# A ring of seven buffers for the residual stream, three chunks of the next tile loaded a tile ahead

## The chip, the cores and the metric

The kernel runs on all 8 cores of one Trainium2 chip. Each core has five engines with an instruction stream of their own: TensorE (PE, matrix multiply), VectorE (DVE), ScalarE (ACT), GpSimd (POOL) and SyncE (SP), which here only issues DMA transfers. A core takes 4 of the 32 prompt sequences and 2 of the 16 sample streams; the cores exchange nothing. The metric is the device time of the slowest core in microseconds (us).

## The reference, cut to what matters

Two layers, each a mixer in two branches, then a normalisation. Biases, the split of `h` and the cache bookkeeping are left out here.

```python
h = x @ w_in                                   # 1024 -> 3072: u, v, g_A | glu_val, glu_gate, g_B
v = LN(gelu(v)) * a_ln_g + a_ln_b
s = tril(W_s[head]) @ v + bias                 # within chunks of 128 positions
y_a = gelu(u) * s * silu(g_A)
a = glu_val * sigmoid(glu_gate)
c = causal_depthwise_conv(a, width=31)
y_b = silu(LN(c)) * silu(g_B)
x_new = LN(ALPHA * x + concat(y_a, y_b) @ w_out)
```

Prompt: 32 sequences of 2048 positions, width 1024, float32. Sample: 16 streams of 32 positions. Outputs are both activations, the last 30 rows of the convolution's input, and the normalised `v` of the sample (`new_av_sample`, which needs `a_ln_g` and `a_ln_b` in full).

## The kernel before

A core works through 16 prompt tiles of 512 positions (4 sequences of 4 tiles), then one sample tile of 64. Each tile passes through both layers before the next begins. `Sched.emit` appends each instruction to its engine's list in the order of the Python code and adds a semaphore wait for whatever buffer it reads or overwrites; a DMA's wait stands in the issuing engine's list. So SyncE's list is strictly in order: what stands behind a waiting DMA waits as well.

A tile lives in four chunks of 128 positions, each a float32 buffer `xres` of 128x1024 (512 KB). Both layers update it in place: it is the residual, and at the end of layer 1 the result, stored from there to `yp` (L654). The buffers form a ring of five, `chunk_idx(t, j) = (4 * t + j) % 5`.

`tile_layer` does one layer of one tile. First, for each chunk j: ScalarE casts it to bf16 (L397) into `xbf`, which shares its memory with `yT`, so that the first cast waits until the output projection of the layer before has read `yT`; TensorE transposes it in 8 pieces (L400) into one of two PSUM buffers `ptr`; and VectorE (even j, L409) or ScalarE (odd j, L406) copies it to `xT`. When all four are there, the input projection runs: blocks of 512 output columns, 32 matmuls of 128x512 each (L417, L494), their weights in a ring of four slots `wr`, loaded by SyncE (L371) from a bf16 copy `wsc` that the first tile writes. Behind the first two blocks the convolution's input is spread by 16 small DMAs to `Sb` (L465). Gating, convolution and spatial matmuls follow, and the output projection (L622), chunk by chunk: `wo_front` adds it to the residual (L625) and sums its squares (ScalarE L629, GpSimd), `wo_back`, one chunk later, normalises it on VectorE (L647, L650). In layer 1 `wo_back` also puts the store L654 in SyncE's list.

The x loads (L678) are put in SyncE's list at two places: chunk 0 of tile t+1 ahead of tile t's layers, and chunks 1 to 3 of tile t+1 behind them. A load waits for the store of the chunk that had its buffer last:

```python
if t + 1 < n_tiles:
    emit_xload(t + 1, [0])
...                       # both layers of tile t, with its stores
if t + 1 < n_tiles:
    emit_xload(t + 1, [1, 2, 3])
```

`a_ln_g` and `a_ln_b` stand as broadcasts over 128 partitions in `avg` and `avb` (256 KB each a layer), loaded in the prologue (L277). `avb` is used in the prologue (L329), and both in the sample tile (L517, L519) only. `mhalf` holds -0.5 as the exponent of `rsqrt_pool` (L252), which reads at most four columns of it. The prologue loads parameters, builds the convolution's and the spatial weights, then loads the first x chunks.

Of the kernel before, what the change touches and what calls it, by code (L numbers as in the profile page):

```python
# [131 lines left out]
def build_nc(n_seq=4, seq_len=SEQ, n_samp=2):  # L132
# [29 lines left out]
    with es:  # L162
        sb = lambda name, shape, dt=F32: es.enter_context(nc.sbuf_tensor(name, shape, dt))
        S = Sched()
        for n in ["pe", "act", "dve", "pool", "sp", "d_c", "d_w0", "d_w1", "d_w2", "d_w3",
                  "d_s", "d_o0", "d_o1", "d_o2", "d_o3", "d_o4", "d_oc", "d_ov", "d_m", "d_pw0", "d_pw1", "d_pw2", "d_pw3", "d_pm", "d_ws0", "d_ws1", "d_ws2", "d_ws3", "d_x0", "d_x1", "d_x2", "d_x3", "d_x4", "d_m2"]:
            S.add_engine(n, es.enter_context(nc.semaphore("s_" + n)))

        xres = [sb(f"xres{i}", [128, D]) for i in range(5)]
# [20 lines left out]
        mhalf = sb("mhalf", [128, TT])  # L190
# [15 lines left out]
        avg = [sb(f"avg{l}", [128, WA]) for l in range(DEPTH)]  # L206
        avb = [sb(f"avb{l}", [128, WA]) for l in range(DEPTH)]
# [93 lines left out]
        for l in range(DEPTH):  # L301
# [27 lines left out]
            S.emit("dve", lambda e, l=l: e.tensor_copy(out=vbb, in_=avb[l][:]), reads=[f"avb{l}"], writes=CSQ4)  # L329
# [54 lines left out]
        def tile_layer(l, T, segs, xk, first_in_seq, last_in_seq, sample, hist_src, conv_out, y_out, av_out):  # L384
# [123 lines left out]
            for j in range(nj):  # L508
# [4 lines left out]
                if sample:  # L513
# [3 lines left out]
                    S.emit("dve", lambda e: e.tensor_tensor(out=vf32[:PT, :], in0=vf32[:PT, :], in1=avg[l][:PT, :], op=ALU.mult),  # L517
                           reads=["ostage", f"avg{l}"], writes=["ostage"])
                    S.emit("dve", lambda e: e.tensor_tensor(out=vf32[:PT, :], in0=vf32[:PT, :], in1=avb[l][:PT, :], op=ALU.add),  # L519
                           reads=["ostage", f"avb{l}"], writes=["ostage"])  # L520
# [148 lines left out]
        def chunk_idx(t, j):  # L669
            return (4 * t + j) % 5  # L670

        def emit_xload(t, js):
            b = t // tiles_per_seq
            ti = t % tiles_per_seq
            keys = []
            for j in js:
# [4 lines left out]
                keys.append(f"xres{idx}")  # L681
            return keys

        emit_xload(0, [0, 1, 2, 3])
# [101 lines left out]
```

How the kernel before makes its waits and increments, by code:

```python
    def replay(self, eng, handle):  # L113
        E = self.engs[eng]
        for kind, p in E.ops:
            if kind == "wait":
                e, v = p
                handle.wait_ge(self.engs[e].sem, v)
            elif kind == "op":
                p(handle)
            elif kind == "opinc":
                p(handle).then_inc(E.sem, 1)
            else:
                fn, d = p
                fn(handle).then_inc(self.engs[d].sem, 16)
```

## Time and profile before

| | |
|---|---|
| two runs | 3895.09 and 3959.07 us, median 3927.08 |
| the profiled execution | 3747.47 us |
| its span, slowest core (core 6) | 3745.9 us |
| spans of the eight cores | 3712.3 to 3745.9 us |
| busy share of PE, DVE, ACT, POOL | 68%, 39%, 37%, 20% |
| moved by DMA | 451.20 MB, mean 120 GB/s |

The profile shows the slowest core of one execution. A line number such as L397 is that of the kernel before. A row of the timeline has its start, its length, the engine, the line, the operation with the tiles it writes and reads, and in brackets how long the engine was idle before it and what ended that. `SPq` is the issuing of a DMA by SyncE; the transfer itself lasts longer than its issue. The timeline merges neighbours of one kind, with their count (x8).

### The profile page before, as it was taken

Reading aid. Unit: us, or ns where it says so; the run is one execution under the profiler, and the core shown is the slowest. Engines: PE = TensorE matmul, PEld = TensorE weight load, DVE = VectorE, ACT = ScalarE, POOL = GpSimd, SP = SyncE. Lnnn points to the kernel's source line nnn. Section 1 sums busy time; section 2 is a strip of 40 time slices with the busy share of each in tenths; the row PEclk is TensorE's granted clock in tenths of the full one; section 3 lists DMA queues with packets and bytes.
Section 4 is the critical chain, followed back from the end, with each engine's and each line's share of the span. In section 5 each row is a group of like instructions: output and inputs, shape, how many; then the busy total and the mean of one; then the engine's idle time right before and its main releaser. Section 6 shows DMA issues by size and latency. Waiting matters only on the chain.

```text
span 3745.9 us, 47469 instructions; the slowest of 8 cores (3712.3 to 3745.9 us)
## 1 busy us (share of the span) xinstructions
PE 2531.3 (68%) x15728; PEld 1171.4 (31%) x15728; DVE 1449.3 (39%) x2286; ACT 1396.4 (37%) x2285; POOL 752.2 (20%) x1186
## 2 busy tenths in 40 slices
PE   0465776867677676767677776768777677776753
PEld 0232333323233333323333333323333233333322
DVE  0144433334444342444434244443324444342442
ACT  0233444433443343334334343443433343343333
POOL 1032211112222121222212122221112222121221
PEclk9887888877788787878888787878778788887876
DMA  7764334342233434323343433243343333434324
GB/s 104 187 138 156 114 97 153 104 147 92 113 114 103 148 114 137 114 107 98 109 142 114 136 114 120 97 145 94 115 136 96 120 103 109 141 114 134 114 89 135
DMA packets 200509, 451.20 MB, mean 120 GB/s; under 512 B 62828, under 2 KB 147172, under 8 KB 165452
## 3 DMA queue, kind: packets, MB, share of 16 engines
q1 hardware_dynamic: 183436, 431.28, 35.6%
q0 software_dynamic: 16832, 16.90, 3.1%
q8 instruction: 128, 2.10, 0.2%
q14 instruction: 113, 0.93, 0.1%
HBM read 341.59 MB, written 51.59 MB: 105 GB/s over the span
## 4 chain that ended last, share of the span: by engine, by line
PE 50%; ACT 15%; issue 9%; DVE 8%; SPq 7%; DMA 6%; POOL 3%; DVEq 0%; ACTq 0%; POOLq 0%
PE pb L417 29%; PE pb L622 11%; SPq L465 4%; DVE yT L611 3%; PE pb L494 3%; DMA xres<-xp 3%; ACT cT L575 2%; ACT tmpf L629 2%; ACT csq L538 2%; ACT cbf L541 2%; ACT cT L535 2%; PE ptr L400 2%; DMA Sb<-a2T 2%; PE pb L547 2%; DVE xres L625 2%
## 5 line engine op out<-in xcount | busy, mean ns | idle before, releaser
L417 PE MATMUL pb<-xT,wr 128*128 128x512 bf16 (+1 forms) x5440 | 1250.2, 396 | 40.0 <-ACT xT L406 40.0
L417 PEld LDWEIGHTS pb<-xT,wr 128*128 128x128 bf16 x5440 | 544.2, 105 | 741.5 <-issue 239.2
L622 PE MATMUL pb<-wr,yT 128*128 128x512 bf16 (+1 forms) x2080 | 533.1, 424 | 280.2 <-DVE yT L611 276.8
L400 PE MATMUL ptr<-identb,yT 128*128 128x128 bf16 (+1 forms) x1040 | 124.4, 306 | 451.6 <-ACT yT L397 400.0
L629 ACT ACTIVATE tmpf<-xres 128x512 f32<-128x512 f32 x260 | 163.7, 630 | 651.7 <-DVE xres L625 639.0
L622 PEld LDWEIGHTS pb<-wr,yT 128*128 128x128 bf16 (+1 forms) x2080 | 220.4, 107 | 581.5 <-issue 393.8
L565 POOL TENSOR_TENSOR tT<-tT,tmpf 128x512 f32<-128x512 f32 (+1 forms) x136 | 179.2, 1345 | 833.7 <-ACT tmpf L564 833.7
L530 PE MATMUL pb<-Sb,Wst 128*32 128x512 bf16 (+1 forms) x4608 | 238.5, 365 | 102.9 <-DMA Sb<-a2T 59.8
L625 DVE SCALAR_TENSOR_TENSOR xres<-xres,pb 128x512 f32<-128x512 f32 x260 | 178.0, 684 | 322.6 <-PE pb L622 240.1
L503 POOL TENSOR_SCALAR sm<-mv 128x4 f32<-128x4 f32 (+1 forms) x34 | 8.0, 234 | 1406.1 <-DVE mv L501 1406.1
L452 DVE SCALAR_TENSOR_TENSOR a2T<-tmpf,pb 128x512 bf16<-128x512 f32 (+1 forms) x144 | 90.3, 632 | 510.1 <-PE pb L417 509.5
L500 DVE BATCH_NORM_STATS2 st6v<-tmpf 128x6 f32<-128x512 f32 (+1 forms) x130 | 90.3, 694 | 432.3 <-ACT tmpf L499 432.0
L400 PEld LDWEIGHTS ptr<-identb,yT 128*128 128x128 bf16 (+1 forms) x1040 | 101.5, 139 | 482.3 <-issue 481.3
L494 PE MATMUL pb<-wr,xT 128*128 128x512 bf16 (+1 forms) x1040 | 233.4, 383 | 0.0
L553 DVE SCALAR_TENSOR_TENSOR nt_a<-pb,nt_a 128x512 f32<-128x512 f32 (+1 forms) x34 | 22.6, 664 | 481.3 <-PE pb L549 415.2
L487 ACT ACTIVATE sgb<-pb 128x512 f32<-128x512 f32 (+1 forms) x136 | 77.5, 574 | 321.2 <-PE pb L417 321.2
L607 POOL TENSOR_TENSOR yT<-tmpf,tT 128x512 bf16<-128x512 f32 (+1 forms) x136 | 194.3, 1438 | 11.1 <-POOL yT L607 0.9
L397 ACT CAST yT<-xres 128x1024 bf16<-128x1024 f32 (+1 forms) x130 | 132.1, 1041 | 171.1 <-DMA xres<-xp 158.0
L530 PEld LDWEIGHTS pb<-Sb,Wst 128*32 128x32 bf16 x4608 | 122.7, 99 | 218.8 <-issue 122.5
L611 DVE TENSOR_TENSOR yT<-cT,sgb 128x512 bf16<-128x512 f32 (+1 forms) x136 | 185.5, 1383 | 7.7 <-DVE yT L611 0.8
L547 PE MATMUL pb<-cbf,onesb 128*128 128x512 bf16 (+1 forms) x136 | 58.8, 584 | 187.1 <-ACT cbf L541 187.1
L647 DVE SCALAR_TENSOR_TENSOR xres<-xres,psc,pg 128x1024 f32<-128x1024 f32 (+1 forms) x130 | 166.6, 1281 | 35.9 <-POOL psc L641 35.9
(89 smaller groups left out, 2556.9 us busy)
## 6 DMA issues: line engine op xcount, KB each, us to landing
wr<-wsc SPq DMA_DIRECT2D x256, 1024.0 KB, 5.8
Sb<-a2T SPq DMA_DIRECT2D x512, 135.0 KB, 3.1
xres<-xp SPq DMA_DIRECT2D x64, 512.0 KB, 6.3
yp<-xres SPq DMA_DIRECT2D x64, 512.0 KB, 2.7
wsc<-wr SPq DMA_DIRECT2D x16, 1024.0 KB, 11.0
wr<-w_in POOLq DMA_DIRECT2D x12, 1024.0 KB, 15.1
wr<-w_out POOLq DMA_DIRECT2D x4, 1024.0 KB, 17.6
pg<-post_ln_g SPq DMA_DIRECT2D x2, 512.0 KB, 7.0
```

What stands on the lines that cost most here:

```text
L400: S.emit("pe", [(lambda e, j=j, k=k, pi=pi: e.transpose(out=ptr[:, pi, 128 * k:128 * k + PT], in_=xbf[:PT, j, 128 * k:128 * k + 128], iden ...
L417: S.emit("pe", [(lambda e, k=k, m=m, pb=pb, wt=wt: e.matmul(pb[:, 0:T], lhsT=wt[:, k, 128 * m:128 * m + 128], rhs=xT[:, k, 0:T], start=(k ...
L465: S.emit("sp", [(lambda e, s=s, g=g, sg=sg: e.dma_start(out=Sv[32 * s:32 * s + 32, :, sg, 0:ncol].rearrange("p (m f) c -> p m f c", f=4)[: ...
L494: S.emit("pe", [(lambda e, k=k, j=j, pb=pb, wt=wt: e.matmul(pb[:PT, :], lhsT=xT[:, k, 128 * j:128 * j + PT], rhs=wt[:, k, :], start=(k == ...
L530: fns.append(lambda e, m=m, s=s, c0=c0, n=n, mm=mm, g=g, pb=pb: e.matmul(pb[32 * g:32 * g + 32, c0:c0 + n], lhsT=Wst[l][:, 4 * m + g, mm, ...
L565: S.emit("pool", lambda e: e.tensor_tensor(out=tTt[:, m, 0:T], in0=tTt[:, m, 0:T], in1=tp[:, 0:T], op=ALU.mult), reads=[tk, f"tT{m}"], wri ...
L607: S.emit("pool", lambda e, m=m, tp=tp: e.tensor_tensor(out=yT[:, m, 0:T], in0=tp[:, 0:T], in1=tTt[:, m, 0:T], op=ALU.mult), reads=[tk, f"t ...
L611: S.emit("dve", lambda e, m=m: e.tensor_tensor(out=yT[:, 4 + m, 0:T], in0=cT[:, m, 0:T], in1=sgb[:, m, 0:T], op=ALU.mult), reads=[f"cT{m}" ...
L622: S.emit("pe", [(lambda e, k=k, j=j, pb=pb, wt=wt: e.matmul(pb[:PT, :], lhsT=yT[:, k, 128 * j:128 * j + PT], rhs=wt[:, k, :], start=(k == ...
L625: S.emit("dve", lambda e, xr=xr, pb=pb, n2=n2, j=j: e.scalar_tensor_tensor(out=xr[:PT, 512 * n2:512 * n2 + 512], in0=xr[:PT, 512 * n2:512 ...
L629: S.emit("act", lambda e, xr=xr, tp=tp, n2=n2, j=j: e.activation(out=tp[:PT, :], in_=xr[:PT, 512 * n2:512 * n2 + 512], func=AF.Square, acc ...
L647: S.emit("dve", lambda e, xr=xr, j=j: e.scalar_tensor_tensor(out=xr[:PT, :], in0=xr[:PT, :], scalar=psc[:PT, j, 0:1], in1=pg[l][:PT, :], o ...
```

## The change

The ring has seven buffers (`% 7`). Chunks 0, 1 and 2 of tile t+1 are put in SyncE's list ahead of tile t's layers, chunk 3 behind them. To make room (two buffers of 4 KB a partition), the four tiles `avg` and `avb` go (8 KB a partition) and `mhalf` shrinks from 512 to 8 columns. `a_ln_b` is loaded in the prologue into the right halves of buffers 5 and 6, which the loads of chunks 1 and 2 of tile 1 overwrite; both `a_ln_g` and `a_ln_b` are loaded again ahead of the last tile's layers into two free buffers, where the sample tile reads them.

```diff
-        xres = [sb(f"xres{i}", [128, D]) for i in range(5)]
+        xres = [sb(f"xres{i}", [128, D]) for i in range(7)]
-        mhalf = sb("mhalf", [128, TT])
+        mhalf = sb("mhalf", [128, 8])
-        avg = [sb(f"avg{l}", [128, WA]) for l in range(DEPTH)]
-        avb = [sb(f"avb{l}", [128, WA]) for l in range(DEPTH)]
+        av_chunk = [5, 6]
-            pload(avg[l][:], a_ln_g[l].partition_broadcast(128), f"avg{l}")
-            pload(avb[l][:], a_ln_b[l].partition_broadcast(128), f"avb{l}")
+            pload(xres[av_chunk[l]][:, 512:1024], a_ln_b[l].partition_broadcast(128), f"xres{av_chunk[l]}")
...
         def chunk_idx(t, j):
-            return (4 * t + j) % 5
+            return (4 * t + j) % 7
...
             if t + 1 < n_tiles:
-                emit_xload(t + 1, [0])
+                emit_xload(t + 1, [0, 1, 2])
             else:
                 S.emit("sp", lambda e: e.dma_start(out=xres[sidx][0:n_samp * DEC_SEQ, :], in_=xs.rearrange("b t d -> (b t) d")),
                        writes=[f"xres{sidx}"], dma=f"d_x{sidx}")
+                for l in range(DEPTH):
+                    c = chunk_idx(n_tiles, 1 + l)
+                    av_chunk[l] = c
+                    S.emit("sp", [lambda e, c=c, l=l: e.dma_start(out=xres[c][:, 0:512], in_=a_ln_g[l].partition_broadcast(128)),
+                                  lambda e, c=c, l=l: e.dma_start(out=xres[c][:, 512:1024], in_=a_ln_b[l].partition_broadcast(128))],
+                           writes=[f"xres{c}"], dma=f"d_x{c}")
...
             if t + 1 < n_tiles:
-                emit_xload(t + 1, [1, 2, 3])
+                emit_xload(t + 1, [3])
```

Below, SyncE's list at the passage from tile 0 to tile 1, before the change. The number behind `xres` or `wr` is the buffer's; `s_d_o0` is the semaphore of the stores from `xres0`, `s_dve` and `s_pe` are the engines'. Here buffers 0, 1 and 2 take chunks 1, 2 and 3 of tile 1, and buffer 3 takes chunk 0 of tile 2:

```order
L654 DMA yp<-xres0 128x1024 [waits s_dve]
L654 DMA yp<-xres1 128x1024 [waits s_dve]
L654 DMA yp<-xres2 128x1024 [waits s_dve]
L654 DMA yp<-xres3 128x1024 [waits s_dve]
L678 DMA xres0<-xp 128x1024 [waits s_d_o0]
L678 DMA xres1<-xp 128x1024 [waits s_d_o1]
L678 DMA xres2<-xp 128x1024 [waits s_d_o2]
L678 DMA xres3<-xp 128x1024 [waits s_d_o3]
L371 DMA wr2<-wsc 128x4096 [waits s_d_ws2,s_pe]
```

And with the change:

```order
L653 DMA yp<-xres0 128x1024 [waits s_dve]
L653 DMA yp<-xres1 128x1024 [waits s_dve]
L653 DMA yp<-xres2 128x1024 [waits s_dve]
L653 DMA yp<-xres3 128x1024 [waits s_dve]
L676 DMA xres0<-xp 128x1024 [waits s_d_o0]
L676 DMA xres1<-xp 128x1024 [waits s_d_o1]
L676 DMA xres2<-xp 128x1024 [waits s_d_o2]
L676 DMA xres3<-xp 128x1024 [waits s_d_o3]
L369 DMA wr2<-wsc 128x4096 [waits s_d_ws2,s_pe]
```

Row by row it reads the same; what moved is the meaning of the buffers. Buffer 0 now takes chunk 3 of tile 1, and buffers 1, 2 and 3 take chunks 0, 1 and 2 of tile 2. The four loads wait for the same four stores as before, and the weight loads stand behind four of them as before.

ScalarE's list at the same passage, where it casts the chunks of tile 1 (`s_d_x0` is the semaphore of the loads into `xres0`), before the change:

```order
L397 CAST yT<-xres4 128x1024 [waits s_d_x4,s_pe]
L397 CAST yT<-xres0 128x1024 [waits s_d_x0]
L406 COPY xT<-ptr1 128x8x128 [waits s_pe]
L397 CAST yT<-xres1 128x1024 [waits s_d_x1]
L397 CAST yT<-xres2 128x1024 [waits s_d_x2]
L406 COPY xT<-ptr1 128x8x128 [waits s_pe]
```

And with the change:

```order
L395 CAST yT<-xres4 128x1024 [waits s_d_x4,s_pe]
L395 CAST yT<-xres5 128x1024 [waits s_d_x5]
L404 COPY xT<-ptr1 128x8x128 [waits s_pe]
L395 CAST yT<-xres6 128x1024 [waits s_d_x6]
L395 CAST yT<-xres0 128x1024 [waits s_d_x0]
L404 COPY xT<-ptr1 128x8x128 [waits s_pe]
```

The first cast reads buffer 4 in both. Chunks 1, 2 and 3 came from buffers 0, 1 and 2, all loaded at the passage; now chunks 1 and 2 come from buffers 5 and 6, loaded in the prologue, and only chunk 3 from buffer 0, loaded at the passage.

SyncE's list at the end of the prologue (`s_d_c`: parameter loads), before the change:

```order
L678 DMA xres0<-xp 128x1024
L678 DMA xres1<-xp 128x1024
L678 DMA xres2<-xp 128x1024
L678 DMA xres3<-xp 128x1024
L678 DMA xres4<-xp 128x1024
L367 DMA wsc<-wr0 128x4096 [waits s_d_pw0]
```

And with the change:

```order
L676 DMA xres0<-xp 128x1024
L676 DMA xres1<-xp 128x1024
L676 DMA xres2<-xp 128x1024
L676 DMA xres3<-xp 128x1024
L676 DMA xres4<-xp 128x1024
L676 DMA xres5<-xp 128x1024 [waits s_d_c]
L676 DMA xres6<-xp 128x1024 [waits s_dve]
L365 DMA wsc<-wr0 128x4096 [waits s_d_pw0]
```

Two loads are added ahead of the first tile's weight stores, one with a wait for the parameter loads and one with a wait for VectorE.

## Rows read from the trace of the kernel before

**Rows 1.** The page: its head, and the chain that ended last by engine and by line:

```profile
span 3745.9 us, 47469 instructions; the slowest of 8 cores (3712.3 to 3745.9 us)
...
PE 50%; ACT 15%; issue 9%; DVE 8%; SPq 7%; DMA 6%; POOL 3%; DVEq 0%; ACTq 0%; POOLq 0%
PE pb L417 29%; PE pb L622 11%; SPq L465 4%; DVE yT L611 3%; PE pb L494 3%; DMA xres<-xp 3%; ACT cT L575 2%; ACT tmpf L629 2%; ACT csq L538 2%; ACT cbf L541 2%; ACT cT L535 2%; PE ptr L400 2%; DMA Sb<-a2T 2%; PE pb L547 2%; DVE xres L625 2%
```

**Rows 2.** List of waits: engine, line, waited for, us in total, times, longest:

```profile
ACT yT L397 <- DMA xres<-xp: 158.0, 15, 11.5
```

**Rows 3.** Timeline of one passage: start, us, engine, line, tiles, [idle before, releaser]:

```profile
763.68 9.44 PE L622 MATMUL pb<-wr,yT 128*128 128x512 bf16 x43
...
777.84 1.03 ACT L397 CAST yT<-xres 128x1024 bf16<-128x1024 f32 x1
...
782.13 1.29 DVE L650 SCALAR_TENSOR_TENSOR xres<-xres,sm,pbb 128x1024 f32<-128x1024 f32 x1 [0.17 <-POOL a2T L438]
783.33 0.69 DVE L409 COPY xT<-ptr 128x1024 bf16<-128x1024 bf16 x1
783.91 2.87 SPq L678 DMA_DIRECT2D xres<-xp  x4
786.94 1.37 SPq L371 DMA_DIRECT2D wr<-wsc  x2
790.40 1.04 ACT L397 CAST yT<-xres 128x1024 bf16<-128x1024 f32 x1 [11.54 <-DMA xres<-xp]
...
791.59 1.01 PE L400 MATMUL ptr<-identb,yT 128*128 128x128 bf16 x8 [11.57 <-ACT yT L397]
792.69 1.01 ACT L406 COPY xT<-ptr 128x1024 bf16<-128x1024 bf16 x1 [1.25 <-PE ptr L400]
...
796.86 1.01 ACT L406 COPY xT<-ptr 128x1024 bf16<-128x1024 bf16 x1 [1.26 <-PE ptr L400]
...
798.01 4.42 PE L417 MATMUL pb<-xT,wr 128*128 128x512 bf16 x10 [1.25 <-ACT xT L406]
```

**Rows 4.** Timeline from layer 0 to layer 1 of one tile:

```profile
667.64 3.62 PE L622 MATMUL pb<-wr,yT 128*128 128x512 bf16 x16
...
685.42 4.94 PE L417 MATMUL pb<-xT,wr 128*128 128x512 bf16 x12 [1.25 <-ACT xT L406]
```

**Rows 5.** Timeline: first passage's cast; last passage's cast and first matmul:

```profile
364.06 1.04 ACT L397 CAST yT<-xres 128x1024 bf16<-128x1024 f32 x1 [11.42 <-DMA xres<-xp]
...
3403.54 1.04 ACT L397 CAST yT<-xres 128x1024 bf16<-128x1024 f32 x1 [10.12 <-DMA xres<-xp]
...
3411.16 16.91 PE L417 MATMUL pb<-xT,wr 128*128 128x512 bf16 x64 [1.25 <-ACT xT L406]
```

**Rows 6.** X loads (L678), issue to landing: all 64, then one passage's four:

```profile
DMA to landing us min/median/max: 4.5/6.3/8.9
...
DMA to landing us min/median/max: 6.4/7.4/7.7
```

**Rows 7.** Timeline of TensorE: the first 96 matmuls after two passages:

```profile
1236.65 22.24 PE L417 MATMUL pb<-xT,wr 128*128 128x512 bf16 x96 [1.25 <-ACT xT L406]
...
1449.06 23.54 PE L417 MATMUL pb<-xT,wr 128*128 128x512 bf16 x96 [1.25 <-ACT xT L406]
```

**Rows 8.** Stretch of the first tile: engines' busy us, clock, DMA share, GB/s:

```profile
113.00:135.00 22.00, 13.84 (x67) 7.15 (x68) 2.69 (x3) 9.32 (x11) 0.00 (x0) 1.00 0.76 309
```

**Rows 9.** Timeline of the prologue: a broadcast, VectorE's bias copy, the x loads:

```profile
15.94 0.43 SPq L277 DMA_DIRECT2D avg<-a_ln_g  x1
...
107.13 0.42 DVE L329 CAST csq<-avb 128x512 bf16<-128x512 f32 x1
...
108.64 4.41 SPq L678 DMA_DIRECT2D xres<-xp  x5
```

**Rows 10.** The two weight loads behind the x loads of [rows 3], to landing:

```profile
DMA to landing us min/median/max: 11.2/12.0/12.9
```

**Rows 11.** Spans and mean granted clock of the cores:

```profile
core 6: 3745.9 us, clock 0.816
```

More of the change, by code:

```diff
@@ L165, in build_nc @@
         for n in ["pe", "act", "dve", "pool", "sp", "d_c", "d_w0", "d_w1", "d_w2", "d_w3",
-                  "d_s", "d_o0", "d_o1", "d_o2", "d_o3", "d_o4", "d_oc", "d_ov", "d_m", "d_pw0", "d_pw1", "d_pw2", "d_pw3", "d_pm", "d_ws0", "d_ws1", "d_ws2", "d_ws3", "d_x0", "d_x1", "d_x2", "d_x3", "d_x4", "d_m2"]:
+                  "d_s", "d_o0", "d_o1", "d_o2", "d_o3", "d_o4", "d_o5", "d_o6", "d_x5", "d_x6", "d_oc", "d_ov", "d_m", "d_pw0", "d_pw1", "d_pw2", "d_pw3", "d_pm", "d_ws0", "d_ws1", "d_ws2", "d_ws3", "d_x0", "d_x1", "d_x2", "d_x3", "d_x4", "d_m2"]:
             S.add_engine(n, es.enter_context(nc.semaphore("s_" + n)))
-        xres = [sb(f"xres{i}", [128, D]) for i in range(5)]
+        xres = [sb(f"xres{i}", [128, D]) for i in range(7)]
         yT = sb("yT", [128, 8, TT], BF16)
@@ L328, in build_nc @@
                           for s2 in range(2)], reads=[f"WmT{l}"], writes=[f"WmTs{l}_0", f"WmTs{l}_1"], dma="d_m2")
-            S.emit("dve", lambda e, l=l: e.tensor_copy(out=vbb, in_=avb[l][:]), reads=[f"avb{l}"], writes=CSQ4)
+            S.emit("dve", lambda e, c=av_chunk[l]: e.tensor_copy(out=vbb, in_=xres[c][:, 512:1024]), reads=[f"xres{av_chunk[l]}"], writes=CSQ4)
             pbk, pkk = next_bank()
@@ L516, in tile_layer @@
                            reads=[tk, "sm1", "sm4"], writes=["ostage"])
[L517 to L520, printed above, removed]
+                    avc = av_chunk[l]
+                    S.emit("dve", lambda e, avc=avc: e.tensor_tensor(out=vf32[:PT, :], in0=vf32[:PT, :], in1=xres[avc][:PT, 0:512], op=ALU.mult),
+                           reads=["ostage", f"xres{avc}"], writes=["ostage"])
+                    S.emit("dve", lambda e, avc=avc: e.tensor_tensor(out=vf32[:PT, :], in0=vf32[:PT, :], in1=xres[avc][:PT, 512:1024], op=ALU.add),
+                           reads=["ostage", f"xres{avc}"], writes=["ostage"])
                     S.emit("sp", [(lambda e, s=s, c0=c0, n=n: e.dma_start(out=av_out[s], in_=vf32[c0:c0 + n, :]))
@@ L674, in emit_xload @@
             ti = t % tiles_per_seq
-            keys = []
             for j in js:
@@ L680, in emit_xload @@
                     writes=[f"xres{idx}"], dma=f"d_x{idx}")
-                keys.append(f"xres{idx}")
-            return keys
         emit_xload(0, [0, 1, 2, 3])
-        sidx = (4 * n_tiles) % 5
+        sidx = chunk_idx(n_tiles, 0)
         for t in range(n_tiles):
@@ L709, in build_nc @@
                        [nav[l, s] for s in range(n_samp)])
-        S.wait_all("sp", ["d_o0", "d_o1", "d_o2", "d_o3", "d_o4", "d_oc", "d_ov", "d_ws0", "d_ws1", "d_ws2", "d_ws3", "d_m", "d_m2", "d_s", "d_x0", "d_x1", "d_x2", "d_x3", "d_x4", "d_c", "d_pm"])
+        S.wait_all("sp", ["d_o0", "d_o1", "d_o2", "d_o3", "d_o4", "d_o5", "d_o6", "d_x5", "d_x6", "d_oc", "d_ov", "d_ws0", "d_ws1", "d_ws2", "d_ws3", "d_m", "d_m2", "d_s", "d_x0", "d_x1", "d_x2", "d_x3", "d_x4", "d_x5", "d_x6", "d_o5", "d_o6", "d_c", "d_pm"])
         with nc.allow_non_contiguous_dma(reason="tiny parameter gathers in the prologue"):
```

## The prediction

> **What bounds the kernel now.** I read the chain of work that ended last first. TensorE holds 50% of it, but one share is a plain transfer: loads of x (`DMA xres<-xp`), 3% of 3745.9 us [rows 1]. The list of waits says who stands there: ScalarE's cast at L397 waits 158.0 us in 15 waits, 11.5 us at the longest, for those loads [rows 2]. There are 16 prompt tiles, so 15 passages from one to the next: one wait for each, 10.5 us on average.
>
> The timeline of one passage shows its shape [rows 3]. TensorE's last matmul of the output projection ends at 763.68 + 9.44 = 773.12. The cast of chunk 0 runs at 777.84, since chunk 0 was loaded a tile ahead. Chunks 1 to 3 are asked for only at 783.91, because SyncE's queue is in order and they stand behind the fourth store of y, which needs VectorE's L650 of chunk 3 (it runs until 783.42). Chunk 1's cast starts at 790.40, 6.49 us after the request, with 11.54 us of idle before it. From there a serial tail runs: transposes, copy L406 at 792.69, the casts of chunks 2 and 3, transposes, copy at 796.86, and the first matmul of the next block at 798.01, 7.61 us after chunk 1's cast. The gap on TensorE's big matmuls is 24.89 us. The last passage repeats it: cast at 3403.54 after 10.12 us of idle, first matmul at 3411.16, again 7.62 us later; the first passage waits 11.42 us [rows 5]. From layer 0 to layer 1 inside a tile, where nothing is loaded, the gap is 685.42 - (667.64 + 3.62) = 14.16 us [rows 4]. So at most 24.9 - 14.2 = 10.7 us a passage, 160 us in all, hangs on the loads, and only if all of them were hidden.
>
> **The change, part by part.** *The ring of seven.* Chunks 0, 1 and 2 of the next tile are now loaded a whole tile ahead. Chunk 3 still stands behind the fourth store, but it is now the first of four loads there, in the place that chunk 1 had. The number of loads at that point of the queue is the same (four), and so is what they wait for, as the order shows. Weights for blocks 2 and 3 behind them are issued no later. So the passage becomes: casts of chunks 0 and 1 at 777.84 and right after it; chunk 1's copy on ScalarE; chunk 2's cast; VectorE's copy of chunk 0 at 783.33 as before (it is behind L650), then chunk 2's transposes and copy, about 1.9 us more (8 transposes take 792.69 - 791.59 = 1.10, a VectorE copy 0.69), done by 786. All of that is over before chunk 3 lands. I take chunk 3's cast to start where chunk 1's does now, 790.40. Behind it are the cast with its hand-over 791.59 - 790.40 = 1.19, transposes 1.10, and copy with hand-over 798.01 - 796.86 = 1.15 [rows 3], together 3.44 us in the place of 7.61. The gain is 4.17 us a passage, x 15 = 62.5 us.
>
> How sure is "lands where chunk 1 does"? The four loads of this passage took 6.4 to 7.7 us each from issue to landing, and all 64 took 4.5 to 8.9 [rows 6]. Four loads issued within 2.87 us with nearly one duration could mean that they share the engines evenly, so that the first gains nothing by being first. Bounds: landing 7.7 us after the request in place of 6.4 leaves 4.17 - 1.3 = 2.9 us a passage (43 us); 8.9 leaves 1.7 us (25 us). At best it comes after 4.5 us. Chunk 1's cast started 6.49 us after the request here, and on average 1.0 us sooner, since the mean wait is 10.5 us against 11.54 here; so 5.5 - 4.5 = 1 us more a passage (78 us). I take the middle, since contents and order of that stretch of the queue are unchanged. The Trainium skill, "DMA: Bandwidth & Descriptors", section "Queues, rings and completion order", says that each DMA engine takes descriptors in the order of its ring, but that a later transfer may finish before an earlier one. By its first half chunk 3 inherits chunk 1's place and the sum is the 62 us; by its second half the 43 us would be possible.
>
> *The clock at the start of the next block.* The first 10 matmuls after the passage take 4.42 us, 0.44 each [rows 3], the lower of the two levels (1.2 GHz); whole blocks of 96 take 22.24 to 23.54 us [rows 7]. What precedes a block now is 24 transposes in the last 7 us, afterwards only 8. No row shows a full-width block after so few. So the clock may rise later. Below: nothing. Above: the 1.3 us between the two blocks of [rows 7] at each passage, 20 us. I take 0.5 us, x 15 = 7.5 us lost, since both blocks of [rows 7] already begin slow after a gap.
>
> *Prologue.* Seven x loads stand there in place of five: +1 MB, early, while the first tile waits for its weights. From 113 to 135 us the queues moved 309 GB/s [rows 8], so 1 MB is 3.4 us of transfer; nothing if it fits between others, 3.4 if the weights wait behind all of it. I take 3. Two broadcasts of `a_ln_g` go away, 0.43 us of issue each [rows 9]: -1. The seventh load waits for the copy of `a_ln_b` in VectorE's prologue, which starts at 107.13, before SyncE issues the first x load at 108.64 [rows 9], so nothing; the smaller `mhalf` is read by the same few columns, so nothing.
>
> *The last tile.* In place of three x chunks and the sample's, it now issues one chunk, the sample's, and four broadcasts. That is less data before the weights; the broadcasts' issue time stands ahead of blocks 2 and 3. Those weights, issued from 786.94 on [rows 3], landed 11.2 to 12.9 us later [rows 10], so by 801; block 2 starts two thirds of 23.5 us after 798, at 814, and at 810 with the change. Cover 9 us; nothing charged, in any tile.
>
> Sum: 62.5 - 7.5 - 3 + 1 = 53 us. The profiled execution took 3747.47 us, so it would become about 3694. The two runs shown have the median 3927.08, 4.8% higher, for the same program; passages are made of ScalarE work and transfers, so I carry the 53 us over unscaled: **3874 us**, 1.4% less.
>
> **Rivals.**
> - *All of the load wait goes* (chance 0.04): gap 14.2 as between layers, 160 us less, 3767. Against it: chunk 3 is requested behind the fourth store, at 783.9, when the first matmul would already be near.
> - *No gain* (0.12): chunk 3 lands so late, or the clock rises so late, that under 20 us are left, 3910 to 3930. Landing at 8.9 us with the whole 1.3 us of clock gives 25 - 20 = 5 us. For it: the even durations of the four loads. Against it: in-order issue, and chunk 1 did come first.
> - *Slower* (0.07): TensorE's granted clock sinks because its work is packed more densely. Place: the matmul blocks, 50% of the chain, 1873 us, at a mean granted clock of 0.816 [rows 1, 11]. One per cent off that clock costs 19 us, so it decides from 2.8% on and is slower by 2% (79 us) from 7%. For it: the same program already ran 148 and 212 us above the profiled execution. Against it: the gap only shrinks from 24 to 20 us, and TensorE's work per us rises by 1.4%. The Trainium skill, "TensorE: Matmul & The Clock Gate", section "Seeing it yourself", warns of a current limiter that lowers a die's clock when several of its cores run dense matmuls; that would act this way. No row here shows it at work.
> - *The level of the runs moves* (0.13): a run of the changed kernel near the profiled execution's level gives 3694, whatever the ring does.
> - *My forecast*, a gain of 20 to 78 us at the level shown: 0.64.
>
> **The numbers.** At the level of the two runs the forecast's own range is 3849 to 3907, widened by their spread (3895 to 3959, 32 either way of the median). The lower end must reach the profiled level with the gain, 3680; the upper takes in the smallest gain, 3908. About 2% is what a measurement of this kernel can tell from no change. Faster by over 2%: 0.04 for the hidden wait, most of the level rival, and a little of the forecast's edge, 0.18. Slower by over 2%: the clock rival and some of a level that moves up, 0.07. Within: 0.75.
>
> **What would show it.** In the changed profile the cast's waits for x are 15 still, but of about 7 us each in place of 10.5 (the casts of chunks 1 and 2 and a copy, 3 us, and a hand-over have moved ahead of them); the wait is followed by one transposing round and the first matmul 3.4 us later, and the gap on big matmuls is near 20 us. A gap of 24 would say that chunk 3 comes late; a first block over 24 us, that the clock took it; a first tile longer by over 5 us, that the prologue cost more. I am wrong if the four loads land together or the granted clock differs by over 2%.

## The result

The changed kernel takes 3719.43 us in the median of 11 runs, the kernel before 3827.77 us in the median of 10. In about half of the runs of either kernel at least one die ran at a lower mean granted clock and held the time up; the comparison leaves such runs out, and all that follows leaves out such runs or such dies. It gives a ratio of 0.9753, 95% interval 0.9728 to 0.9778: faster by 2.5%. The profiled executions are 3747.47 us before and 3651.53 us after, 96 us less, where 53 us were forecast.

The page of the changed kernel, to be read beside [rows 1]: its head, and the chain by engine and by line. A line number of the changed kernel is one to two lower here than that of the same statement before (L395 for L397, L415 for L417, L676 for L678).

```profile
span 3650.0 us, 47476 instructions; the slowest of 8 cores (3620.0 to 3650.0 us)
...
PE 51%; ACT 15%; issue 9%; DVE 8%; SPq 7%; DMA 5%; POOL 4%; ACTq 0%; DVEq 0%; POOLq 0%
PE pb L415 31%; PE pb L621 11%; SPq L463 4%; DVE yT L610 3%; PE pb L492 3%; ACT cT L574 3%; DMA xres<-xp 2%; ACT tmpf L628 2%; ACT cT L534 2%; ACT csq L537 2%; ACT cbf L540 2%; DMA Sb<-a2T 2%; SPq L310 2%; DVE xres L624 2%; PE pb L546 2%
```

Its slowest core, beside [rows 11]. The mean granted clock of the slowest core rose from 0.816 to 0.831, and the mean over the eight cores from 0.821 to 0.833:

```profile
core 0: 3650.0 us, clock 0.831
```

The cast's wait for x, beside [rows 2]: still 15 waits, but 6.2 us each in place of 10.5:

```profile
ACT yT L395 <- DMA xres<-xp: 92.8, 15, 7.7
```

The timeline of one passage, beside [rows 3]:

```profile
1384.06 16.32 PE L621 MATMUL pb<-wr,yT 128*128 128x512 bf16 x64 [8.46 <-DVE yT L610]
...
1405.10 1.97 ACT L395 CAST yT<-xres 128x1024 bf16<-128x1024 f32 x2
...
1409.23 1.05 ACT L395 CAST yT<-xres 128x1024 bf16<-128x1024 f32 x1
1409.40 1.28 DVE L649 SCALAR_TENSOR_TENSOR xres<-xres,sm,pbb 128x1024 f32<-128x1024 f32 x1 [0.17 <-POOL a2T L436]
1410.60 0.68 DVE L407 COPY xT<-ptr 128x1024 bf16<-128x1024 bf16 x1
1411.18 2.92 SPq L676 DMA_DIRECT2D xres<-xp  x4
...
1416.00 1.04 ACT L395 CAST yT<-xres 128x1024 bf16<-128x1024 f32 x1 [5.72 <-DMA xres<-xp]
...
1417.18 1.01 PE L398 MATMUL ptr<-identb,yT 128*128 128x128 bf16 x8 [4.74 <-ACT yT L395]
1418.29 1.01 ACT L404 COPY xT<-ptr 128x1024 bf16<-128x1024 bf16 x1 [1.25 <-PE ptr L398]
...
1419.44 5.77 PE L415 MATMUL pb<-xT,wr 128*128 128x512 bf16 x18 [1.25 <-ACT xT L404]
```

The output projection ends at 1384.06 + 16.32 = 1400.38 and the next block starts at 1419.44, a gap of 19.06 us where [rows 3] had 24.89. Chunks 0 and 1 are cast at 1405.10 and chunk 2 at 1409.23, before SyncE issues its four loads at 1411.18. Only chunk 3 is waited for. Its cast starts 4.82 us after the request, and the first matmul 3.44 us behind the cast: exactly the tail that the forecast had made of [rows 3].

From the timelines of all eight cores, the sums over the 15 passages and the tiles behind them (mean over the cores, us):

| part | before | after | after - before |
|---|---|---|---|
| first tile, both layers | 345.4 | 341.0 | -4.4 |
| gap at the passage | 357.5 | 291.9 | -65.6 |
| layer 0: first 96 matmuls and what stands among them | 367.2 | 354.6 | -12.6 |
| layer 0: from there to the statistics' matmuls, with them | 363.1 | 362.9 | -0.2 |
| layer 0: second block, spatial matmuls, waits | 366.5 | 364.7 | -1.8 |
| layer 0: output projection | 241.1 | 239.0 | -2.1 |
| layer 1, all of it | 1552.0 | 1546.5 | -5.5 |
| sample tile | 126.0 | 125.9 | -0.1 |

So 66 of 92 us are the gap, and 22 us come out of stretches that the change does not touch, 12.6 of them out of the first matmul blocks, which have the same instructions and now take less time. The other 4 us are the first tile's.

A view that the forecast had not used shows how. These are the issues of the y stores by SyncE, one group at the end of each tile, so their distances are the time from tile to tile. Before, at the ends of tiles 3 to 6 (counted from 0):

```profile
995.14 13.92 SPq L654 DMA_DIRECT2D yp<-xres  x4
...
1210.46 13.61 SPq L654 DMA_DIRECT2D yp<-xres  x4
...
1421.86 13.92 SPq L654 DMA_DIRECT2D yp<-xres  x4
...
1636.82 13.92 SPq L654 DMA_DIRECT2D yp<-xres  x4
```

215.3, 211.4 and 215.0 us. And after:

```profile
980.97 13.93 SPq L653 DMA_DIRECT2D yp<-xres  x4
...
1188.96 13.92 SPq L653 DMA_DIRECT2D yp<-xres  x4
...
1397.16 13.93 SPq L653 DMA_DIRECT2D yp<-xres  x4
...
1605.36 13.92 SPq L653 DMA_DIRECT2D yp<-xres  x4
```

208.0, 208.2 and 208.2 us. Times of ordinary tiles (those that do not end a sequence; 88 on the eight cores) do not spread evenly. Before, 54 are nearest to 215.0 and 30 to 211.6 us; after, 73 to 208.2 and 13 to 211.6. They move in steps of 3.4 us.

### The profile page after: what moved, and what is told of

It is laid out like the page before. It is cut to its first block, busy times and chain, and to the rows that moved or that the text cites. A ratio compares the mean times of both kernels' runs of the same rounds, so it can differ in the third digit from the quotient of the medians.

```text
span 3650.0 us, 47476 instructions; the slowest of 8 cores (3620.0 to 3650.0 us)
## 1 busy us (share of the span) xinstructions
PE 2498.8 (68%) x15728; PEld 1163.1 (32%) x15728; DVE 1451.4 (40%) x2286; ACT 1395.9 (38%) x2285; POOL 753.9 (21%) x1186
## 4 chain that ended last, share of the span: by engine, by line
PE 51%; ACT 15%; issue 9%; DVE 8%; SPq 7%; DMA 5%; POOL 4%; ACTq 0%; DVEq 0%; POOLq 0%
PE pb L415 31%; PE pb L621 11%; SPq L463 4%; DVE yT L610 3%; PE pb L492 3%; ACT cT L574 3%; DMA xres<-xp 2%; ACT tmpf L628 2%; ACT cT L534 2%; ACT csq L537 2%; ACT cbf L540 2%; DMA Sb<-a2T 2%; SPq L310 2%; DVE xres L624 2%; PE pb L546 2%
## 5 line engine op out<-in xcount | busy, mean ns | idle before, releaser
L415 PE MATMUL pb<-xT,wr 128*128 128x512 bf16 (+1 forms) x5440 | 1227.0, 391 | 40.0 <-ACT xT L404 40.0
L415 PEld LDWEIGHTS pb<-xT,wr 128*128 128x128 bf16 x5440 | 538.9, 104 | 723.9 <-issue 188.9
L398 PE MATMUL ptr<-identb,yT 128*128 128x128 bf16 (+1 forms) x1040 | 125.9, 306 | 386.1 <-ACT yT L395 286.4
L649 DVE SCALAR_TENSOR_TENSOR xres<-xres,sm,pbb 128x1024 f32<-128x1024 f32 (+1 forms) x130 | 167.7, 1290 | 24.2 <-POOL psc L632 16.9
```

The source lines that it names most:

```text
L398: S.emit("pe", [(lambda e, j=j, k=k, pi=pi: e.transpose(out=ptr[:, pi, 128 * k:128 * k + PT], in_=xbf[:PT, j, 128 * k:128 * k + 128], iden ...
L415: S.emit("pe", [(lambda e, k=k, m=m, pb=pb, wt=wt: e.matmul(pb[:, 0:T], lhsT=wt[:, k, 128 * m:128 * m + 128], rhs=xT[:, k, 0:T], start=(k ...
L649: S.emit("dve", lambda e, xr=xr, j=j: e.scalar_tensor_tensor(out=xr[:PT, :], in0=xr[:PT, :], scalar=sm[1][:PT, j:j + 1], in1=pbb[l][:PT, : ...
```

## The experiments

Theory A: the gain comes from when chunks are asked for. Theory K: beside that, the blocks' time depends on where a stretch of matmuls begins against changes of the granted clock that come at their own times, so tile times move in steps and a gap's change does not show as itself. Rivals: the memory layout does it; the clock simply comes back sooner after a shorter gap (S); time is simply added and taken away (L). The experiments ran on four chips; the kernel before, run again on each, had medians of 3739 to 3748 us there. Differences between two experiments are therefore read from the times of tiles and blocks first. Three of the kernels below rest on one execution each (four copies on the changed kernel, eight copies, two copies with the filler), two on two each (the early load without copies and with two), and one on four cores of one execution.

### The ring and the prologue alone

To the changed kernel, with the loads put back in their old places:

```diff
-                emit_xload(t + 1, [0, 1, 2])
+                emit_xload(t + 1, [0])
...
-                emit_xload(t + 1, [3])
+                emit_xload(t + 1, [1, 2, 3])
```

> Seven buffers and the new prologue, but the loads of x at the two old places (chunk 0 of the next tile ahead of the layers, chunks 1 to 3 behind them). Theory A (the gain comes from when chunks are asked for, plus the clock; the prologue gives its own 4.6 us): the passages between tiles are as in the kernel before, big-matmul gap near 23.8 us, 15 waits of the cast of about 10.5 us; the first x load is issued about 4.6 us earlier than before on average over the cores; time 0.998 of before. Rival B (the memory layout or the ring's size itself speeds something up, such as the first matmul block): the first block of 96 matmuls is shorter by 0.8 us at each passage with the gap unchanged, time 0.99 of before.

Ratio to before 0.9994 (0.9971 to 1.0017). The row of the cast's wait:

```profile
ACT yT L395 <- DMA xres<-xp: 156.7, 15, 11.8
```

The sum of the gaps is 355.8 us (before 357.5), that of the first blocks 367.0 (before 367.2). So the seven buffers, their addresses and the smaller tiles do nothing that shows at the passages, and rival B falls. The first x load is issued at 100.7 us on average over the cores, against 107.0 before. But in the other runs with the new prologue this average lies anywhere from 99.7 to 108.2 us, and in the one other run with the old prologue at 105.4. The first tile takes anywhere from 337 to 346 us in the runs with the new prologue, and 345 and 342 us in the two with the old one. The 4.4 us of the table are inside that spread, so whether the prologue gains anything stays open.

### Five buffers, loads between the stores

Each load of chunk j stands right behind the store of chunk j. To the kernel before:

```diff
                     S.emit("sp", lambda e, xr=xr, j=j: e.dma_start(out=y_out[j], in_=xr[:PT, :]), reads=[xkey], dma="d_o" + xkey[-1])
+                    after_store(j)      # emit_xload(t + 1, [j]) for j >= 1
...
-            if t + 1 < n_tiles:
-                emit_xload(t + 1, [1, 2, 3])
```

> The kernel before with its five buffers and its prologue; only each load of chunk j (1, 2, 3) of the next tile now stands right behind the store of chunk j, in place of all three behind the fourth store. Theory A (what counts is that one chunk alone is still asked for behind the fourth store): gap near 19.5 us as in the changed kernel, time 0.976 to 0.98 of before. Rival C (the two more buffers are needed, since a load waits for the landing of a store just issued): gap stays over 22 us, time 0.99 to 1.0 of before.

Ratio 0.9807 (0.9749 to 0.9865), where rival C had said 0.99 to 1.0. One passage of it, SyncE, ScalarE and TensorE (L660 is the store, L685 the load, L403 the cast, L423 the first block):

```profile
991.64 0.33 SPq L660 DMA_DIRECT2D yp<-xres  x1
992.07 3.19 SPq L685 DMA_DIRECT2D xres<-xp  x2
...
998.68 1.05 ACT L403 CAST yT<-xres 128x1024 bf16<-128x1024 f32 x1 [3.98 <-DMA xres<-xp]
...
1002.13 23.26 PE L423 MATMUL pb<-xT,wr 128*128 128x512 bf16 x96 [1.25 <-ACT xT L412]
```

The last store is issued at 991.64, chunk 3's load right behind it, its cast runs at 998.68, and the block starts 3.45 us later. The mean gap is 19.8 us. The mechanism of the forecast is shown, and it does not need the two buffers: what counts is how many chunks stand behind the fourth store. The rival, a wait for a store just issued, costs little: 45 waits of the cast for x with 106.1 us in all, where the changed kernel has 15 with 92.8. Of 88 ordinary tiles 49 take 208.2 us and 38 take 211.6. With a gap larger by 0.3 us than in the changed kernel, 25 more tiles stand on the higher step.

### Chunk 3 asked for early as well

To the changed kernel, the load of chunk 3 right behind the second store; it needs the buffer of the first:

```diff
+                    after_store(j)      # emit_xload(t + 1, [3]) for j == 1
...
-            if t + 1 < n_tiles:
-                emit_xload(t + 1, [3])
```

> The changed kernel, with the load of chunk 3 right behind the second store of y (it needs the first one's buffer) in place of behind the fourth. Theory A: no chunk is waited for any more, the gap falls to the 14.2 us that stand between the two layers of a tile, 5.3 us less than in the changed kernel at 15 passages, 80 us: ratio to before near 0.955. If the clock's rise is a matter of where a stretch of matmuls begins (theory K), the 80 us come out as anything from 51 to 102 us, a whole number of steps of 3.4 us at most passages; if the clock comes back sooner only because the gap is shorter (theory S), the first block of 96 matmuls also loses another 1.0 us, 95 us in all. Rival: the load collides with the weights' and makes the next block wait; gap at 14.2 but a later block longer.

Two of its executions can be compared, 3603 and 3605 us, beside 3729 to 3749 us for the kernel before on the same chip: about 3.6% less, without an interval. One passage (L683 the load, L401 the cast, L421 the block):

```profile
970.79 0.38 SPq L683 DMA_DIRECT2D xres<-xp  x1
...
977.47 1.99 ACT L401 CAST yT<-xres 128x1024 bf16<-128x1024 f32 x2
...
982.79 22.50 PE L421 MATMUL pb<-xT,wr 128*128 128x512 bf16 x92 [1.25 <-ACT xT L410]
```

The load is issued at 970.79, the casts of chunks 2 and 3 run together at 977.47 with no wait for x, and none is left in the list of waits. The gap is 14.2 us at every passage, the floor that [rows 4] gave. But 79.2 us less gap brought only 52.7 us in layer 0, and layer 1 took 15.3 us more. The first block of a layer shows part of it:

```profile
1392.59 23.27 PE L421 MATMUL pb<-xT,wr 128*128 128x512 bf16 x96 [1.25 <-ACT xT L410]
```

In an ordinary tile the first 96 matmuls now take 23.15 us on average, against 22.5 us in the changed kernel. The tiles stand at 204.8 us (79 of 88), and those that end a sequence at 218.4 us, all 32, against 216.4 on average in the changed kernel. SyncE's second group of stores at the ends of tiles 4 to 7, two distances of ordinary tiles and that of the last one of a sequence:

```profile
1180.10 4.02 SPq L659 DMA_DIRECT2D yp<-xres  x2
...
1385.11 4.02 SPq L659 DMA_DIRECT2D yp<-xres  x2
...
1589.70 4.02 SPq L659 DMA_DIRECT2D yp<-xres  x2
...
1808.25 4.02 SPq L659 DMA_DIRECT2D yp<-xres  x2
```

205.0, 204.6 and 218.6 us. Theory S said that a shorter gap makes the first block shorter; it is longer. The rival of a collision with the weights falls too: on none of the eight cores does the list of waits have TensorE waiting for a load into `wr`. The forecast of 0.955 was too good. With 53 us in layer 0 theory K's band of 51 to 102 us holds; with layer 1 the gain is 37 us, and the band is missed.

### Delays in the passage

Copies on ScalarE between the last transposes and the copy to `xT`, two or four, to the changed kernel and to the one with the early load:

```diff
+                if j == 3 and l == 0 and pad_on[0]:      # pad_on[0] = t > 0
+                    for _ in range(2):                   # 4
+                        S.emit("act", lambda e: e.copy(out=nt_a[:, 0:TT], in_=nt_a[:, 0:TT]), reads=[pk, "nt_a"], writes=["nt_a"])
```

> The changed kernel with two added ScalarE copies of 128x512 (about 0.6 us each) in each of the 15 passages, between the last chunk's transposes and its copy to xT, so that the gap grows from 19.5 to about 20.8 us. Theory K (what the clock adds or takes depends on when a stretch begins, in steps): the time from tile to tile takes the same few values as in the changed kernel (208.1, 211.5, 215 us), most tiles unchanged or 3.4 us longer; the added 1.2 us does not show as 1.2. Theory S (a longer gap means a later clock, smoothly): every tile is longer by 1.2 plus 0.3 us, 22 us in all.

Ratio to before 0.9908 (0.9876 to 0.9939), where the changed kernel has 0.9753. Stores of three ordinary tiles:

```profile
1189.49 13.92 SPq L657 DMA_DIRECT2D yp<-xres  x4
...
1401.14 13.93 SPq L657 DMA_DIRECT2D yp<-xres  x4
...
1612.84 13.93 SPq L657 DMA_DIRECT2D yp<-xres  x4
```

211.65 and 211.70 us: 75 of 88 ordinary tiles stand at 211.6, 13 at 208.2. The gap grew by 1.5 us and an ordinary tile by 2.5, the 15 passages with their tiles by 46 us in all, where theory S had said 22 and simple adding of the 1.5 us would give 23.

> The changed kernel with four added copies, 2.5 us, in each passage: gap near 22.0 us, where the changed kernel has 19.6 and the one with two copies 21.0. Theory K: ordinary tiles at 211.4 us, the same as with two copies, so twice the delay costs no more. Theory L: 1.2 us more a tile than with two copies, 212.6.

```profile
1199.68 13.92 SPq L657 DMA_DIRECT2D yp<-xres  x4
...
1411.30 13.92 SPq L657 DMA_DIRECT2D yp<-xres  x4
...
1622.91 13.92 SPq L657 DMA_DIRECT2D yp<-xres  x4
```

211.62 and 211.61 us. With a gap of 22.4 us in place of 21.0 an ordinary tile takes 211.9 us in place of 211.1. The first 1.5 us of delay cost 2.5 us, the next 1.4 us cost 0.9. By the mean alone this lies between theory K (0) and theory L (1.2) and decides nothing; the split speaks for K, with 78 tiles at 211.6, 10 at 215.0 and none at 212.6.

> The kernel with the early load of chunk 3 (gap 14.2 us, 204.8 us from tile to tile), and two added ScalarE copies, 1.23 us, in each of the 15 passages, between the last transposes and the copy to xT. Theory K (steps): over the earlier runs the ordinary tiles took 204.8 us at a gap of 14.2, 208.1 at 18 to 19.5, 211.3 at 20.5 to 22 and 214.8 us from 23.5 on, so a step lies every 3.4 us of gap and the next one below 19.7 should be near 16.3. A gap of 15.4 stays below it: 204.8 us as without the copies, 0 us in all, the first block of 96 matmuls shorter by about as much as the copies add or later stretches so. Theory L (time is simply added): 206.0 us a tile, 18 us in all.

```profile
1186.18 4.03 SPq L663 DMA_DIRECT2D yp<-xres  x2
...
1390.97 4.03 SPq L663 DMA_DIRECT2D yp<-xres  x2
...
1595.74 4.03 SPq L663 DMA_DIRECT2D yp<-xres  x2
...
1807.92 4.02 SPq L663 DMA_DIRECT2D yp<-xres  x2
```

204.8 us from tile to tile, as without the copies (86 of 88 there), and 212.2 us for the tile that ends the sequence, where the kernel without copies needs 218.6. Mean: 204.7 and 214.1 us against 204.4 and 218.4. The span of the slowest core is 3600.4 us against 3603.7: 18 us of added work, nothing lost. Theory L falls for this kernel.

> The same with four added copies, 2.5 us, gap 16.7 us. Theory K: just past the step expected near 16.3, so 208.1 us for most ordinary tiles, 3.4 us more than without copies; tiles whose gap comes out below it stay at 204.8. Theory L: 207.3 us a tile.

Read on cores 0 to 3: gap 16.8 us, 40 of 44 ordinary tiles at 208.2 us, 4 at 204.8. The step that the earlier runs had placed near 16.3 us is there.

All ordinary tiles of these runs together, by their gap (mean over eight cores; the fourth column counts tiles by the nearest of the values 3.4 us apart; "1.2 us" and "2.5 us" are the added copies):

| kernel | gap, us | tile, us | tiles at the steps |
|---|---|---|---|
| early chunk 3 | 14.2 | 204.4 | 201.4: 9, 204.8: 79 |
| early chunk 3, 1.2 us | 15.4 | 204.7 | 201.4: 2, 204.8: 86 |
| early chunk 3, 2.5 us (4 cores) | 16.8 | 207.8 | 204.8: 4, 208.2: 40 |
| changed kernel | 19.5 | 208.6 | 204.8: 2, 208.2: 73, 211.6: 13 |
| five, interleaved | 19.8 | 209.6 | 204.8: 1, 208.2: 49, 211.6: 38 |
| changed, 1.2 us | 21.0 | 211.1 | 208.2: 13, 211.6: 75 |
| changed, 2.5 us | 22.4 | 211.9 | 211.6: 78, 215.0: 10 |
| seven, loads at the old places | 23.7 | 213.8 | 208.2: 1, 211.6: 27, 215.0: 60 |
| before | 23.8 | 213.8 | 208.2: 2, 211.6: 30, 215.0: 54, 218.5 and more: 2 |

### Delay only where it helps

> The kernel with the early load of chunk 3, and two added ScalarE copies, 1.23 us, only in the passage into the last tile of each of the 4 sequences. With the copies in every passage these tiles took 214.1 us, without any 218.4 us, and the ordinary tiles 204.7 and 204.4 us. Theory K (steps): 214 us for the last tiles and 204.4 for the others, so about 17 us less than without copies, a span near 3585 us, ratio to before near 0.958. Theory L (time is simply added): 5 us more than without copies, 3608 us. Rival M (the faster last tiles depend on how the tile before them lay against the clock, and that one had copies too): last tiles anywhere from 214 to 218.4 us.

The same two copies, with `pad_on[0] = t % 4 == 3`. Ratio to before 0.9606 (0.9586 to 0.9626). The last tiles take 214.3 us, the others 204.5; the slowest core 3595.8 us, 8 us less than without copies, the mean over the cores 12 us less. Rival M falls: the last tile does as well when the tiles before it have no copies. The 15 tiles gained 16 us, as forecast (17); the first tile took 4 us more in this execution, which is inside that tile's spread.

> The kernel with the early load of chunk 3, and eight added copies, 5.0 us, in the passage into the last tile of each of the 4 sequences only. Over the earlier runs these tiles took 218.4 us at a gap of 14.2 (all 32 of them) and 215.2 us at 19.0 to 19.5 us (30 of 35). Theory K: the added work makes these four tiles shorter, by 3.2 us each, 13 us in all. Theory L: they are longer by 5.0 us each, 20 us in all.

The same eight copies, 5.0 us, with the same `pad_on[0]`. 24 of 32 last tiles take 215.4 us or less, 7 take about 222, the mean is 216.9: 1.5 us less than without 5 us of copies, where 3.2 less were expected (theory L: 5 more). Right in sign; the 7 tiles on a higher step were not foreseen.

### The clock held up

To the kernel with the early load, matmuls with constant operands while TensorE would idle, into a PSUM buffer that the next real matmul overwrites:

```diff
+        def filler(n, l):
+            i = bank_i[0] % 6
+            if n:
+                S.emit("pe", [(lambda e, i=i, l=l: e.matmul(banks[i][:, 0:512], lhsT=onesb[:], rhs=WmT[l][:, 0:4, :],
+                                                            start=True, stop=True)) for _ in range(n)],
+                       reads=["onesb", f"WmT{l}"], writes=[f"pb{i}"])
...
+                if not sample and fill_on[0] and j in (0, 2):     # fill_on[0] = t > 0 or l > 0
+                    filler(20 if j == 0 else 10, l)
                 pi, pk = next_ptr()
...
+            if not sample:
+                filler(24, l)                                     # the second kernel only
             yTk = [f"yT{k}" for k in range(8)]
```

> The kernel with the early load of chunk 3, and TensorE kept at work in the gap before each layer's input projection: 20 matmuls of 128x512 with constant operands behind the output projection and 10 more ahead of chunk 2's transposes, where the engine idles 5.9 and 3.2 us; they write a PSUM buffer that the next real matmul overwrites, so the result is unchanged. Theory K (the 3.4 us steps and the slow start of the first block are the clock's): the first block of 96 matmuls falls from 23.1 us to about 21.0, in every tile, the granted clock stays high over the gap, and the tiles no longer take values 3.4 us apart; 2.1 us less in each of 31 layers and the last tiles' 30 us blocks shorter by more, 80 to 110 us in all, a span near 3500 us. Theory N (the steps come from something else, such as the transfers): the first block stays at 23 us and the steps at 204.8. Rival: the filler delays the transposes or the chip answers denser work with a lower clock on a whole die, no faster.

Ratio to before 0.9363 (0.9337 to 0.9389), 3501 to 3513 us, where theory K had said near 3500. Its profiled execution took 3804.61 us, so its blocks are not read, and what this filler does inside a layer is read from the next two kernels.

> The same, and 24 more such matmuls ahead of each output projection, where TensorE waits 8.5 to 9.2 us for VectorE. Theory K: the output projection's 64 matmuls fall from 16.3 us to about 14.0, 2.3 us in each of 32 layers, 70 us more, a span near 3430 us. If the clock has already fallen when the filler starts, 24 slow matmuls take 10.3 us and delay the projection by up to 2 us instead.

Ratio 0.927 (0.9253 to 0.9287), the fastest kernel of this study; its span is 3473 us where near 3430 was forecast. Head of its page, and the granted clock in its 40 slices, in tenths:

```profile
span 3473.4 us, 50903 instructions; the slowest of 8 cores (3448.6 to 3473.4 us)
...
PEclk9998999999999999999999999999999999999976
```

TensorE on its slowest core over one layer (L359 is the filler, L432 the first block, L640 the output projection):

```profile
1339.49 4.48 PE L359 MATMUL pb<-WmT,onesb 128*128 128x512 bf16 x20
...
1346.94 2.32 PE L359 MATMUL pb<-WmT,onesb 128*128 128x512 bf16 x10
...
1353.01 22.36 PE L432 MATMUL pb<-xT,wr 128*128 128x512 bf16 x96 [1.25 <-ACT xT L421]
...
1423.57 15.66 PE L640 MATMUL pb<-wr,yT 128*128 128x512 bf16 x64 [3.33 <-DVE yT L627]
```

The gap's filler at 1339.49 takes 0.22 us a matmul, so the clock is up. Over all ordinary tiles the first block takes 21.04 us in layer 0 and 21.05 in layer 1, where it took 23.15 without filler and with nearly the same gap (13.4 us here, 14.2 there), as forecast. The block in the rows above, 22.36 us, is one of the minority that still begin at the lower clock. The output projection takes 15.1 to 15.4 us where it took 16.2, less than half of the gain that was forecast (in the last row it waits another 3.33 us behind its filler, and takes 15.66 us). So the slow start of the first block is the clock's, and theory N falls. Theory K had also said that the steps would go, and they have not: of 88 ordinary tiles 35 take 193.8 to 194.9 us and 40 take 197.4 to 198.8, the other 13 lie between. The clock still falls elsewhere in a layer: the projection of layer 0 takes 14.0 us in 28 tiles and 15.7 in 60.

> The kernel with the filled gap, and the two added ScalarE copies, 1.23 us, in each of the 15 passages. Without the filler these copies cost 0.3 us in an ordinary tile and shortened the last tile of a sequence by 4.4 us. Theory K: with the clock held up there is no timing to slip against, so the copies cost what they last, 1.2 us a passage in ordinary and last tiles alike, 18 us in all. Theory N: they cost nothing, as before, and shorten the last tiles.

Neither theory has it. This kernel took 3545 us in its one execution, 32 to 44 us more than the filled one without copies, where 18 were expected. In layer 0, where the copies stand, the first block takes 22.5 us, in layer 1 21.3: ScalarE's copies lengthen the last idle stretch, behind all the filler. The trace's record of the granted clock has 65 of the 88 ordinary blocks of layer 0 begin at the upper level and fall to the lower one about 1 us later; in layer 1, 69 of 88 never leave the upper level. Here a delay cost its time and more; it was no longer free.

## Why the prediction was right or wrong

**What the passage is made of: right.** Chunk 3 alone is waited for, the tail behind its cast is 3.44 us, the weights behind the loads are not late, and all of it without a wait in new places. The gap was forecast to shrink by 4.17 us and shrank by 65.6 / 15 = 4.37. "Lands where chunk 1 does" held: on the slowest core the cast starts 4.8 to 6.8 us after the request, and before it started 4.6 to 6.5 us after. The lower bounds (43 and 25 us) were not needed.

**The clock at the start of the next block: wrong in sign.** This is the step that failed. The forecast took 7.5 us of loss, from the idea that fewer transposes ahead of a block can only delay the clock, with zero as the best case. Measured is a gain: 12.6 us in the first blocks, 22 us with the later stretches and layer 1. The rows to see it were there. [Rows 7] has two blocks with the same instructions, 22.24 and 23.54 us long, behind gaps made of the same work, and I took the 1.3 us between them for a bound on a cost, not for a sign that this time is set by when the block begins. The granted clock in one-microsecond stretches shows what it is. Before, behind the passage whose first matmul starts at 1449.06 (columns as in [rows 8]):

```profile
1451.00:1452.00 1.00, 1.00 (x3) 0.29 (x2) 0.00 (x0) 0.00 (x0) 0.00 (x0) 0.50 0.00 0
...
1453.00:1454.00 1.00, 1.00 (x4) 0.30 (x3) 0.00 (x0) 0.38 (x1) 0.00 (x0) 0.50 0.00 0
```

And after, behind the passage whose first matmul starts at 1419.44:

```profile
1421.00:1422.00 1.00, 1.00 (x4) 0.33 (x3) 0.00 (x0) 0.00 (x0) 0.00 (x0) 0.50 1.06 393
...
1423.00:1424.00 1.00, 1.00 (x7) 0.42 (x5) 0.00 (x0) 0.60 (x1) 0.00 (x0) 1.00 0.77 311
```

Before, the clock is still at the lower level (0.50, 1.2 GHz) 4 to 5 us into the block. After, it is at the upper one (1.00, 2.4 GHz) from 3.6 us on, though fewer transposes came ahead. That is one pair. The trace's record of the granted clock, read for the first block of layer 0 in the ordinary tiles, says the same of all:

| kernel | us at the lower level in the block | first 96 matmuls, us |
|---|---|---|
| before | 4.6 | 23.07 |
| changed | 3.7 | 22.51 |
| early chunk 3 | 5.0 | 23.15 |
| early chunk 3, 1.2 us | 3.7 | 22.52 |
| filler in both places | 0.8 | 21.04 |

A block's time follows the time that it spends at the lower level, by about half a microsecond for each, and that time does not follow the length of the gap. The stretch at the lower level that holds the start of this block comes in a few lengths only: 23.9 us in 53 and 27.3 us in 35 of the 88 ordinary tiles before; 17.1 us in 25, 20.5 in 56 and 23.9 in 7 after; 13.7 us in 13 and 17.1 in 75 with the early load. They are 3.4 us apart, as the tile times are. So the clock answers a change at the passage in steps.

A tile's time moved by a step of 3.4 us or two, not by 4.2: from 211.6 and 215.0 to 208.2. That 4.4 us of gap turned into 5.2 us a tile in ordinary tiles (213.8 to 208.6) and 7.6 in the last tiles (224.0 to 216.4) is where these tiles happened to stand. With the early load the same effect took back 42 of 79 us, 27 in layer 0 and 15 in layer 1. In the terms of the forecast's sum, over the eight cores: the gap gave 66 us and not 62.5, the first blocks and the later stretches, where the sum had its term for the clock, 22 and not -7.5, the first tile 4 and not -2. Of the 39 us between 53 and 92, 30 are missing in the clock's term.

**The prologue: not decided.** 3 us of loss against 1 of gain were forecast, 4.4 us of gain measured, within the spread of that stretch from run to run.

**The last tile and the memory: right**, nothing charged and nothing seen (sample tile 126.0 and 125.9 us).

**The level of the runs.** The 3874 us stood on the median of the two runs shown, 3927; against the profiled execution the sum said 3694, and it measured 3651.5. That the median of 3719 lies in the forecast's range of 3680 to 3908 is luck: the range was widened to hold both the profiled execution and those two runs, and five of the eleven runs took 3648 to 3661 us, below it. In the forecast's own terms: 53 us said, 96 measured, 2.5% and not 1.4%, so the likeliest class (within 2%) missed.

The clock was in the list of rivals only as a loss on a whole die; the mean granted clock of the slowest core rose from 0.816 to 0.831 instead. The limiter meant there is the one that the Trainium skill describes ("TensorE: Matmul & The Clock Gate", section "Seeing it yourself"). The forecast said that no row shows such a limiter; the record of the granted clock of the trace before does hold a level of 0.81, for 116 us on core 6 and 113 us on core 7, all between 2668 and 2830 us. Without these two cores the first blocks still gain 12.1 us. The Trainium skill, "TensorE: Matmul & The Clock Gate", section "What's actually happening", says that the clock is throttled by default, is released by activity, and that the changes fall on a time base that runs on by itself. The few lengths of the stretches above agree with that last part, and it would have given a rival with gains and losses in steps.

## What to carry to other kernels

Count what stands in an in-order queue behind the last store of a tile: loads put between the stores brought about four fifths of this gain with five buffers (1.9% of 2.5%, with an interval of 1.4 to 2.5%), and one more moved load hid the rest. Where TensorE idles a few microseconds before each block, a change in its idle time is not worth its own length; look at the spread of tile-to-tile times first, and test with a small delay. If the idle time can't be removed, matmuls whose results nobody reads can be worth as much as the prefetch: with the early load and the filler in one gap or two this kernel runs 6.4% and 7.3% below the kernel before, with the early load alone 3.6%, with the change 2.5%. The filler was not run without the early load. How much idle time may be left behind it was not tested by itself; with 3.3 us left on average 60 of the 88 projections of layer 0 took 15.7 us, and with 3.0 us left the other 28 took 14.0.

## What was not expected of the hardware

Time from tile to tile takes values 3.4 us apart over a range of gaps (204.8, 208.2, 211.6, 215.0 us in 88 tiles a kernel, with 79, 73, 75 and 54 of them on one value), and 5 us of added work made the last tile of a sequence 1.5 us shorter, and 1.2 us of added work made it 4.1 us shorter. Holding TensorE busy through the gap takes the slow start out of the first block (23.15 to 21.05 us) but leaves steps elsewhere. What the chip looks at when it changes the clock was not measured.
